# One memory-key head at each of four seams: a fused layer stack on one Trainium2 core

## What is computed

```python
memn = rms_norm(mem, norm_mem)
k = (memn @ wk).reshape(B, M, 4, 128)      # wk: 1024 x 512, one per hybrid layer
q = (hn @ wq).reshape(B, S, 4, 128)
s = einsum('bshd,bmhd->bhsm', q, k) / sqrt(128)
```

## Time and profile before

| | us |
|---|---|
| median of 3 runs | 1216.83 |
| the profiled execution | 1216.67 |
| its span, first to last instruction | 1214.8 |
| PE busy | 1201.3 (99%) |
| DVE busy | 853.7 (70%) |
| ACT busy | 694.9 (57%) |
| POOL busy | 146.8 (12%) |

### The profile page before, as it was taken

The page is one execution under the profiler, slowest core; times in us unless marked ns, Lnnn a source line. Parts: engine busy times, 40 slices in busy tenths (PEclk is TensorE's granted clock), DMA queues, the critical chain, the costliest instruction groups (busy, mean ns, idle before and its releaser), DMA issues.

```text
span 1214.8 us, 19309 instructions
## 1 busy us (share of the span) xinstructions
PE 1201.3 (99%) x7660; PEld 1064.6 (88%) x7660; DVE 853.7 (70%) x1235; ACT 694.9 (57%) x1014; POOL 146.8 (12%) x182
## 2 busy tenths in 40 slices
PE   8999999999999999999999999999999999999997
PEld 8888888888888988888888888888999898999896
DVE  5566665766667898888886777677665667566665
ACT  6444335665555755555555656556676567565554
POOL 1000000300001000000001311431101411101500
PEclk9999999999999999999999999999999999999999
DMA  9544434655554445444453755554354453453331
GB/s 367 214 164 173 173 141 155 226 195 190 197 184 170 169 159 173 161 159 157 157 176 120 289 196 185 197 185 169 132 202 140 139 208 108 147 185 138 135 139 53
DMA packets 31992, 210.35 MB, mean 173 GB/s; under 512 B 3665, under 2 KB 3938, under 8 KB 11042
## 3 DMA queue, kind: packets, MB, share of 16 engines
q1 hardware_dynamic: 30258, 202.12, 46.8%
q0 software_dynamic: 1504, 6.76, 1.5%
q10 hardware_dynamic: 144, 0.26, 0.1%
HBM read 208.08 MB, written 1.05 MB: 172 GB/s over the span
## 4 chain that ended last, share of the span: by engine, by line
PE 93%; DVE 3%; ACT 2%; issue 1%; DMA 1%; POOL 0%; SPq 0%; DVEq 0%; ACTq 0%; POOLq 0%
PE pair L757 18%; PE pair L639 15%; PE pair L641 15%; PE pair L640 15%; PE pair L751 10%; PE bank L639 3%; PE bank L640 3%; PE bank L641 3%; PE bank L867 1%; PE pair L741 1%; PE bank L1041 1%; PE bank L1050 1%; ACT whi L1466 1%; DVE wlo L2009 1%; PE bank L1063 1%
## 5 line engine op out<-in xcount | busy, mean ns | idle before, releaser
L2009 DVE TENSOR_TENSOR wlo<-raw,whi 128x2048 fp32r<-128x2048 f32 (+2 forms) x195 | 426.6, 2194 | 153.8 <-ACT whi L1466 153.1
L1466 ACT ACTIVATE whi<-raw 128x2048 fp32r<-128x2048 f32 (+2 forms) x195 | 357.4, 1836 | 172.8 <-PE pair L641 143.0
L757 PE MATMUL pair<-ahl,whi 128*128 128x512 f32 x832 | 208.8, 391 | 0.0
L757 PEld LDWEIGHTS pair<-ahl,whi 128*128 128x128 f32 x832 | 153.0, 188 | 29.5
L639 PE MATMUL pair<-whi,bhl 128*128 128x512 f32 (+3 forms) x416 | 150.7, 362 | 1.3 <-ACT arena L1705 1.2
L641 PE MATMUL pair<-whi,bhl 128*128 128x512 f32 (+3 forms) x416 | 146.0, 351 | 0.0
L640 PE MATMUL pair<-wlo,bhl 128*128 128x512 f32 (+3 forms) x416 | 145.8, 351 | 0.0
L751 PE MATMUL pair<-ahl,wlo 128*128 128x256 f32 x832 | 115.1, 282 | 0.0
L751 PEld LDWEIGHTS pair<-ahl,wlo 128*128 128x128 f32 x832 | 110.5, 191 | 3.8
L639 PE MATMUL pair<-whi,ahl 128*128 128x512 f32 (+3 forms) x288 | 109.0, 378 | 0.0
L641 PE MATMUL pair<-whi,ahl 128*128 128x512 f32 (+3 forms) x288 | 106.0, 368 | 0.0
(11 more groups left out here) (338 smaller groups left out, 1967.7 us busy)
## 6 DMA issues: line engine op xcount, KB each, us to landing
raw<-wstream_d SPq DMA_DIRECT2D x161, 1024.0 KB, 4.8
raw<-wstream_d SPq DMA_DIRECT2D x26, 768.0 KB, 4.4
raw<-wstream_d SPq DMA_DIRECT2D x4, 832.0 KB, 5.2
raw<-wstream_d SPq DMA_DIRECT2D x4, 800.0 KB, 4.4
gain_row<-rows_d POOLq DMA_DIRECT2D x5, 512.0 KB, 4.1
arena<-mem_cols_d POOLq DMA_DIRECT2D x2, 1024.0 KB, 8.0
raw<-wstream_d SPq DMA_DIRECT2D x2, 576.0 KB, 3.9
raw<-wstream_d SPq DMA_DIRECT2D x2, 512.0 KB, 6.1
```

The lines of the kernel that those rows point to most:

```text
L757: mm = pe.matmul(pair[:, p, f, :], whi[:, slot, sl], both, start=False, stop=k == KD - 1, skip_group_check=True)
L1466: act.activation(whi[:, n % RING, 0:width[n]], raw[:, n % RAW, 0:width[n]], ACT.Copy).then_inc(hi_ready, 1)
L2009: dve.tensor_tensor(wlo[:, n % RING, 0:width[n]], raw[:, n % RAW, 0:width[n]], whi[:, n % RING, 0:width[n]].bitcast(F32), ALU.subtract).th ...
```

## The change

The keys of layer 0 are taken out of seam 4 and computed one head at a seam, heads 3, 2, 1, 0 at seams 1 to 4, in 24 matmuls each, from a chunk of 128x1024 that now lies in the weight stream at each seam. The identity fills are gone. The memory's columns are loaded four times (four DMAs of 1 MB from POOL's queue in place of one), scaled and split each time in the stage before. A second change stands in the dilated attention: for the last pair, ACT reads the values before a weight split and not behind it, and DVE does its softmax maximum first.

```diff
+            def seam_keys(seam, *cuts):
+                hi, lo, k0 = mem_rows_of[seam]
+                p, c = begin_block("a"), w.chunk
+                slot = c % RING
+                w.chunk += 1
+                def some(first, last):
+                    for k in range(first, last):
+                        if k == 0:
+                            pe.wait_ge(lo_ready, c + 1)
+                        if k % 2 == 0:
+                            pe.wait_ge(mem_lo, 4 * seam + k // 2 + 1)
+                        sl = slice(k * MEM_HD, (k + 1) * MEM_HD)
+                        mm = product(pair[:, p, 0, 0:SEQ], whi[:, slot, sl], wlo[:, slot, sl], hi[:, k0 + k, :], lo[:, k0 + k, :], k == 0, k == KD - 1)
+                        if k == KD // 2 - 1:
+                            mm.then_inc(keys_half, 1)
+                        elif k == KD - 1:
+                            mm.then_inc(chunk_used, 1)
+                return [lambda a=a, b=b: some(a, b) for a, b in zip((0,) + cuts, cuts + (KD,))]
...
             def ffn(l):                                # PE, seams 1 and 3
-                turn_rows(added, (4, 9, 0), held=held)
+                turn_rows(added, seam_keys(2 * l, 3, 6), held)
...
-            aside = next_pair()                        # PE, seam 2
-            keep_warm(aside, 18)
-            pe.wait_ge(post_ready, 2 + 4)
-            turn_rows(added, (0, 2, 0), aside, held)
+            keys, more, rest = seam_keys(1, 7, 7)
+            def sums_weighed():
+                keys()
+                pe.wait_ge(post_ready, 2 + 4)
+            turn_rows(added, (sums_weighed, more, rest), held)
...
+                if l == 0:                             # PE, seam 4
+                    keys, more, rest = seam_keys(3, 7, 7)
+                    ready = turn_rows(added, (sums_weighed, more, rest))
+                    tokens("v", ahi, alo, lhs_ready=ready, between=[nothing, nothing, nothing, spread_rows])
...
-            used(4)                                    # ACT, before seam 1
+            for g in range(KD // 2):
+                used(1)
+                mem_high(0, g)
             ret_out(RET_HEADS - 1)
             used(RET_KT // 2 - 6)
-            passed()
+            used(1)
+            act.wait_ge(mem_lo, 4)
             post_squares(in_pairs=True)
...
             def ffn(l):                                # ACT, seams 1 and 3
-                split_hi(w.chunk - 2)
-                rows_out([(ahi, 0)], [COLS["norm_ffn_pre"] + l * KD], True)
+                rows_out([(ahi, 0)], [COLS["norm_ffn_pre"] + l * KD], True, keys=2 * l)
+                passed()
+                read_keys(2 * l)
                 row_squares(added)
                 catch_up()
...
                     used(1)                            # ACT, dilated pairs
                     passed()
-                    catch_up()
+                    if b < PAIRS - 1:
+                        catch_up()
                     if b >= 2:
                         act.wait_ge(pair_mixed, b - 1)
                     read_values(d_v[b % 2])
+                    catch_up()
...
             for l in range(DEPTH):                     # ACT, seam 4 (l == 0)
-                row_squares(added if l == 0 else summed)
-                catch_up()
-                passed()
-                catch_up()
+                if l: ...
                 rows_out([(ahi, 0)], [COLS["norm_mix_2"] + l * KD])
                 passed()
...
+                else:
+                    p, n = read_keys(3)
+                    row_squares(added)
                 act.wait_ge(drained_a[p], n)
```

More of the change, by code:

```diff
@@ L53 @@
 MEM_H, MEM_HD = 4, 128
+SEAM_HEADS = (3, 2, 1, 0)
 EPS = 1e-6
@@ L80, in weight_blocks @@
     blocks.append(("out", "ret_w_out", 0, r(D), r(RET_KT)))
+    key_blocks = lambda l, heads: [("block", "mem_wk_2", l, np.concatenate([r(MEM_HD) + h * MEM_HD for h in heads]), r(KD))]
+    blocks += key_blocks(0, SEAM_HEADS[0:1])
     def ffn(layer):
@@ L840, in summed, with turn_rows @@
                     pe.wait_ge(*sums_read[t])
[L842 to L856, removed]
+            def seam_keys(seam, *cuts):
[16 more added lines that the diff above has]
+                return [lambda a=a, b=b: some(a, b) for a, b in zip((0,) + cuts, cuts + (KD,))]
+            def turn_rows(x_there, aside=(nothing, nothing, nothing), held=None):
                 base = w.at("turn")
@@ L1146, in _, with sums_weighed @@
             for l in range(DEPTH):
-                ready = []
-                def turn_first():
-                    if l == 0:
+                if l == 0:
+                    keys, more, rest = seam_keys(3, 7, 7)
+                    def sums_weighed():
+                        keys()
                         pe.wait_ge(post_ready, 2 * (2 + 4))
[L1153 to L1158, removed]
+                    ready = turn_rows(added, (sums_weighed, more, rest))
+                    tokens("v", ahi, alo, lhs_ready=ready, between=[nothing, nothing, nothing, spread_rows])
+                else:
+                    ready = []
+                    rows_there = lambda a, b: pe.wait_ge(mem_lo, 4 * 4 + b // 2)
+                    features("a", bhi, blo, k0=KD, lhs_ready=rows_there, between=[nothing, nothing, lambda: ready.append(turn_rows(summed))])
+                    ready = ready[0]
+                    tokens("v", ahi, alo, lhs_ready=ready, between=[spread_rows])
                 pe.wait_ge(spread_out, w.at("spread"))
@@ L1523, in turn_out, with rows_out @@
                 mm.then_inc(turned_hi, 1)
-            def rows_out(dst, gain, each=False, classes=False):
+            def rows_out(dst, gain, each=False, classes=False, keys=None):
                 for g in range(KD // 2):
+                    if keys is not None and g == 0:
+                        act.wait_ge(keys_half, keys + 1)
+                    elif keys is not None and g == KD // 4:
+                        act.wait_ge(chunk_used, w.chunk + 1)
                     turn_out(dst, (2 * g, 2 * g + 1), gain, bank[:, g, :], each, classes)
@@ L1568, in _, with mem_high, read_keys @@
             first_hi(2, 1)
+            def mem_high(n, g):
+                hi, _, k0 = mem_rows_of[n]
+                act.wait_ge(mem_in_sem, 16 * (n + 1))
+                for k in (2 * g, 2 * g + 1):
+                    gc = COLS["norm_mem_2"] + n // 4 * KD + k
+                    ins = act.activation(hi[:, k0 + k, :], mem_t[n][:, k, :], ACT.Copy, scale=cols[:, gc:gc + 1])
+                ins.then_inc(mem_hi, 1)
+            def read_keys(seam):
+                p, n, _ = w.next_block("a")
+                act.activation(e_kT[:, SEAM_HEADS[seam], :], pair[:, p, 0, 0:SEQ], ACT.Copy).then_inc(drained_a[p], 1)
+                return p, n
             def ret_out(h):
@@ L1751, in _ @@
             dil_pt(c, 1)
+            mem_high(2, 3)
             catch_up()
-            w.chunk += 1
+            passed()
+            catch_up()
+            act.wait_ge(mem_lo, 4 * 3)
             post_squares(in_pairs=True)
@@ L1767, in _ @@
             for l in range(DEPTH):
[L1768 to L1772 removed]
+                if l:
+                    row_squares(summed)
+                    catch_up()
+                    passed()
+                    catch_up()
                 rows_out([(ahi, 0)], [COLS["norm_mix_2"] + l * KD])
                 passed()
[L1775 to L1776 removed]
+                if l:
+                    p, n, _ = w.next_block("a")
+                    act.activation(e_kT.rearrange("p (a b) m -> p a (b m)", a=2), pair[:, p, :, :], ACT.Copy).then_inc(drained_a[p], 1)
+                else:
+                    p, n = read_keys(3)
+                    row_squares(added)
                 act.wait_ge(drained_a[p], n)
@@ L2221, in _ @@
             ret_decay(RET_HEADS - 1)
+            mem_low(0, 0)
             used(1)
             ret_norm(RET_HEADS - 1, g_at[RET_HEADS - 1])
-            used(2)
+            mem_low(0, 1)
+            used(1)
+            mem_low(0, 2)
+            used(1)
             ret_out(RET_HEADS - 1)
+            mem_low(0, 3)
             used(RET_KT // 2 - 6)
-            passed()
+            used(1)
             add_post(in_pairs=True)
```

73 lines of the change are left out of this document (45 added, 28 removed).

## The result

The changed kernel takes 1226.56 us (median of 4 runs, 1224.94 to 1227.22), the kernel before 1216.82 us beside it: a ratio of 1.0078, 95% interval 1.0067 to 1.0090. The forecast was slower, 1220.7 us with a range to 1223.5. The direction was right and the size less than half. The profiled execution took 1226.66 us.

A forecast was written before the change was run, and what follows sets the result against it. PE, busy 1201.3 of 1214.8 us, was taken to bound the kernel. Terms 4.1 + 4.1 - 2.8 - 0.3 - 1.2 = +3.9 us gave 1220.7 us, sum range 1218.5 to 1223, 8-in-10 range 1214.5 to 1223.5.

The forecast's parts named there:

- Seams 1 and 3: Entries to both FFNs: U1's split comes late behind rows, key read and squarings, PE idles 2.95 us; each costs 4.1 us.
- the rival that has one: PE's clock falls behind the new gaps near 2.9 us: 1228 us for three falls, 1223 for one; chance 0.1 for any.
- The price of 2.4 us: Cost of one clock fall, taken from the mean granted clock of 0.998 over 1214.8 us before the change.
- Seam 2: Fills and idle time go, A0 starts at 396.65 instead of 397.19: 0.3 us won, bounds 0.6 won and 1.0 lost.
- K and A0 are split 0.4 us sooner: At seam 2, these splits come 0.4 us sooner than those of A0 and Va did; first turn at 394.7, before 395.01.
- Hidden: Scaling and splitting the memory four times costs nothing, since FFN 1 carried those 16 instructions with PE busy throughout.
- Seam 4: Start of the hybrid layer: three heads (8.64 us) given up, G1 starts at 869.4 instead of 872.24; 2.8 us won.
- V2's wait: At seam 4, V2's low half ends at 862.45, so PE starts V2 at 862.5, 2.7 us late.
- the turn's wait: At seam 4, PE idles 1.2 us after 21 key matmuls, until the last weighing is done at 851.3.
- The last pair: Last dilated pair: reading values before the split removes PE's wait on ACT; 1.2 us won, bounds 0.4 and 1.3.
- The early load: First memory load at 25 us, beside the first weight loads: costs 0, with 2 us as upper bound.
- Three times 0.6 us either way: Uncertainty given to each of three stalls, 0.6 us either way; with the early load only adding, 1218.5 to 1223.

The follow-up runs named there:

- e1: Changed kernel, but at seams 1 and 3 ACT splits U1's high half ahead of the eight turned rows: 1215.56 us, ratio 0.9993 to the kernel before.
- f2: Kernel before, but ACT's split for the FFN's second tile falls behind rows and squarings at seams 1 and 3, no key moved: 1225.26 us.
- f1: Changed kernel plus 20 identity transposes on PE between U0 and U1 at seams 1 and 3, splits as late as before: 1223.56 us.
- f3: Kernel of e3, but the scaling of memory rows comes four tiles sooner in either FFN: 1210.45 us, ratio 0.9948 to the kernel before.
- e4: Kernel before with only the last dilated pair's edit: ACT reads values ahead of the weight split, DVE does its maxima first: 1215.51 us.
- e2: Changed kernel, but at seam 4 ACT splits V2's high half ahead of the first hybrid layer's rows: 1222.56 us, ratio 1.0049.
- g1: Kernel of f3, but at seams 1 and 3 DVE's low half of U0 moves behind the additions to x: 1213.21 us, ratio 0.9971.
- e3: Changed kernel with the edits of e1 and e2, and PE spreading the row scale after V2's first half: 1212.18 us, ratio 0.9964.
- g2: Kernel of f3 measured again without any edit, in more rounds: 1210.29 us, ratio 0.9947 to the kernel before.

## Why the prediction was half right

- **Seams 1 and 3 were right**, +4.1 each forecast and measured, step by step: x's addition ended at 206.6 (206.25 forecast), U0 started at 210.0 (209.85), ACT's split of U1 at 214.33 (214.3), U1 at 218.84 (218.6), the stall 2.86 us (2.95). e1 and f2 show that the place of one split in ACT's queue makes the stall; neither the keys nor their loads do.
- **The step that failed** is the clock: the sum has no term for a fall behind a gap, and the rival that has one got "0.1 for any". All three gaps dropped it in the profiled run, and the stretches behind the two at U1 carry 3.6 of the 5.9 us that were missing; a third lies in V2 (1.7). f1 shows that the gap is what drops it. The forecast found no fall in the trace before, but the gaps in it were at most 1.3 us long and could tell nothing of 2.9. The Trainium skill's page "TensorE: Matmul & The Clock Gate" (Part 1) says that the array goes back to half rate when it has stood idle; the traces agree in part, with 0.50 behind eight of the nine traced gaps of 2.1 to 2.9 us and 1.00 behind every one up to 1.8 once the kernel is under way. The price of 2.4 us was too high, for a fall costs 1.8, and it rested on a misreading. The 0.998 was taken for time at the lower level at the start; in the trace before the clock is 1.00 there and falls only after PE's last matmul, which starts at 1207.18:

```profile
1210.00:1211.00 1.00, 0.00 (x0) 0.00 (x0) 0.56 (x2) 0.15 (x1) 0.75 (x1) 0.68 0.00 0
1211.00:1212.00 1.00, 0.00 (x0) 0.00 (x0) 0.54 (x1) 0.57 (x1) 0.00 (x0) 0.50 0.79 324
```

  So that stretch slowed no matmul and gave no price, and it was the one place where the trace before did show the clock falling, some 3 us after PE had stopped.
- **Seam 2 was off in sign**, +0.6 against -0.3 (inside its bounds of -0.6 and +1.0). The step "K and A0 are split 0.4 us sooner" failed: the memory rows that FFN 0 now has in its last tiles put DVE 1.5 us late in the last tile, and the weighing and the turn still came 0.8 to 0.9 us late. "Hidden" was read from PE's busy window, and PE was in fact never stopped inside the FFN; the delay came out behind it. f3 shows it and prices it at 1.7 us for seams 2 and 4 together.
- **Seam 4 was right** without the clock: -2.9 for -2.8, with V2's wait 2.1 for 2.7 and the turn's wait 1.1 for 1.2. Of the 1.11 us that the turn waited 0.9 was the memory work's doing, as f3 shows; the forecast had the wait and not its reason. That the sum came out to 0.1 us is partly luck: counted from the end of FFN 1, V1 started 0.2 us later than forecast, and V2's wait was 0.6 shorter.
- **The last pair was right**: -1.3 in the profile, -1.22 alone (e4).
- **The early load was hidden**, with 0.2 us at most up to seam 1.
- Three times 0.6 us either way is 1218.9 to 1222.5; the range of the sum was given as 1218.5 to 1223. The measured time lies outside both.
- Clock in place, the sum would have been 3.9 + 0.9 (seam 2) + 5.3 (three falls) = 10.1 us, against 9.7 measured.

## What to carry to other kernels

When work is moved in front of an engine that bounds the kernel, write down for each in-order queue beside it what stood in its idle time before, and check that it still does: one split moved by 9 us cost 2.9 us twice, and the clock's 1.8 on top. Price every new gap of 2 us or more on TensorE as the gap plus a possible fall of the clock, 1.8 us here, unless rows of the trace show gaps of that length without one; gaps of 2.1 us brought it in some runs, gaps of 2.9 in every trace that had them. And "the engine stayed busy" clears work inside a stage only; ask also how late it leaves the other queues at the stage's end.

## What the hardware showed that was not expected

- A stretch at 0.50 follows a gap, not always: behind 2.86 and 2.88 us in both profiles that had them (the changed kernel and e2), behind 2.67 but not behind 2.66 us in one run of f2, behind 2.10 to 2.12 in three profiles (the changed kernel, e1, f1), and by the step in the times in 3 of 10 runs of e1. None follows 1.65 us (g1, at both seams) or 1.82 us (f1, 699.67). What decides it in a run is open. It begins at once (e1) to 1.2 us (changed kernel, seam 3) after PE has started again, and each costs 1.7 to 1.8 us.
- Transposes of the identity in a gap are worth having even when PE has nothing to gain from starting sooner: 20 of them (2.35 us) in each of two gaps saved 3.0 us together.
- Some executions have such a stretch from about 8 to 11 us, behind PE's wait for its first weights. It costs nothing: e3 has none, f3 has one, and both start the same matmul at 204.13 us.
- The half clock can hide another wait, and this pair shows it. In e3 PE waits 0.70 us at 14.53 for a low half of the weights; in f3, behind the stretch, it does not. The kernel before, f1 and g1 have no early stretch and wait like e3; the changed kernel, e1, e4, f2 and g2 have one and don't wait. At seam 3 the same is likely for f1 but not shown, and f2 had both, the stretch and a late weight load of 0.9 us.
